# Key chunks of the memory behind the sums of the first two norms, and dense retention products set between the small S5 output products

## The reference

```python
# block 1
u = modulate(x, sh1, sc1); y = swiglu(u, ffn1_w_gate, ffn1_w_up, ffn1_w_down)
x = layer_norm(DEEPNORM_ALPHA * x + FFN_RES_WEIGHT * (1 + g1) * y, ln1_g, ln1_b)       # first norm
u = modulate(x, sh2, sc2); proj = u @ w_in     # recurrent branch, convolution branch, two gates
out = merged @ mix_w_out
x = layer_norm(DEEPNORM_ALPHA * x + (1 + g2) * out, ln2_g, ln2_b)                      # second norm
u = modulate(x, sh3, sc3); y = swiglu(u, ffn2_w_gate, ffn2_w_up, ffn2_w_down)
x = layer_norm(DEEPNORM_ALPHA * x + FFN_RES_WEIGHT * (1 + g3) * y, ln3_g, ln3_b)       # third norm
# block 2
h = rms_norm(x, norm1_g)
q, k, v, g_ret, u, g_s5 = split(h @ w_in_2)
ret = retention(rotary(q), rotary(k), v, ret_gn_g) * silu(g_ret)   # 8 heads, norm over each head
ssm = s5_branch(u, ...) * silu(g_s5)       # linear recurrence with 64 states in 64 groups, then a GLU
x = x + concatenate([ret, ssm]) @ w_out
m = rms_norm(mem, norm_mem_g)              # memory: 256 rows of 1024
ka = m @ xa_wk; va = m @ xa_wv             # keys and values: they depend on the memory alone
x = x + cross_attention(rms_norm(x, norm2_g) @ xa_wq, ka, va) @ xa_wo
return rms_norm(x, norm_f_g)
```

## Time and profile before

| | |
|---|---|
| median of 3 runs | 1992.2 us (1989.76 to 1996.63) |
| the profiled execution | 1996.91 us, of which its span is 1995.1 us |
| TensorE busy | 1895.3 us (95%) |
| VectorE, ScalarE, GpSimd busy | 1072.9, 775.2, 487.0 us |
| moved between device memory and the core | 239.43 MB, mean 120 GB/s |
| mean granted TensorE clock | 0.958 of full speed |

### The profile page before, as it was taken

One profiled execution on the slowest core, in us unless ns is written; L12 is line 12 of the kernel. 1 busy time (PEld: TensorE's weight loads), 2 busy tenths in 40 slices (PEclk: granted clock), 3 DMA queues, 4 the chain that ended last, 5 costly groups with the idle time before them and its releaser, 6 DMA issues.

```text
span 1995.1 us, 23150 instructions
## 1 busy us (share of the span) xinstructions
PE 1895.3 (95%) x8986; PEld 1537.1 (77%) x8986; DVE 1072.9 (54%) x1097; ACT 775.2 (39%) x814; POOL 487.0 (24%) x636
## 2 busy tenths in 40 slices
...
GB/s 302 137 195 173 185 169 157 155 93 85 84 126 127 74 95 148 126 85 64 105 91 98 85 108 87 146 116 192 169 54 156 96 68 46 101 173 90 152 43 43
DMA packets 202773, 239.43 MB, mean 120 GB/s; under 512 B 5611, under 2 KB 184587, under 8 KB 201547
## 3 DMA queue, kind: packets, MB, share of 16 engines
...
## 4 chain that ended last, share of the span: by engine, by line
PE 70%; POOL 9%; DVE 7%; ACT 6%; issue 5%; DMA 1%; SPq 1%; DVEq 0%; POOLq 0%; ACTq 0%
PE ps L2025 22%; PE ps L2214 16%; PE ps L2091 9%; POOL conv_out L481 8%; PE ps L2055 4%; ACT w_hi L603 3%; PE ps L2352 2%; PE ps L2393 2%; PE ps L2530 2%; DVE w_lo L1163 2%; DVE ada_acc L1263 2%; PE ps L2443 1%; PE ps L2431 1%; PE ps L2402 1%; DMA w_raw<-in_ffn_w_gate 1%
## 5 line engine op out<-in xcount | busy, mean ns | idle before, releaser
L1163 DVE TENSOR_TENSOR w_lo<-w_raw,w_hi 128x2048 fp32r<-128x2048 f32 x158 | 369.7, 2340 | 577.2 <-ACT w_hi L603 574.9
L603 ACT ACTIVATE w_hi<-w_raw 128x2048 fp32r<-128x2048 f32 x156 | 298.4, 1913 | 684.3 <-PE ps L2214 235.5
L2025 PE MATMUL ps<-u_hi,w_hi 128*128 128x512 f32 x704 | 279.8, 397 | 5.1 <-DVE w_lo L1163 5.0
L2025 PE MATMUL ps<-u_lo,w_hi 128*128 128x512 f32 x704 | 276.2, 392 | 0.0
L2025 PE MATMUL ps<-u_hi,w_lo 128*128 128x512 f32 x704 | 276.0, 392 | 0.0
L2214 PE MATMUL ps<-u_hi,w_hi 128*128 128x512 f32 x656 | 256.9, 392 | 5.0 <-DVE w_lo L1163 5.0
L2214 PE MATMUL ps<-u_lo,w_hi 128*128 128x512 f32 x656 | 255.8, 390 | 0.0
L2214 PE MATMUL ps<-u_hi,w_lo 128*128 128x512 f32 x656 | 255.8, 390 | 0.0
L481 POOL TENSOR_TENSOR conv_out<-conv_out,conv_tap 128x512 f32<-128x512 f32 x120 | 195.4, 1628 | 92.9 <-ACT conv_tap L745 75.9
L2025 PEld LDWEIGHTS ps<-u_hi,w_hi 128*128 128x128 f32 x704 | 133.7, 190 | 37.1 <-issue 7.5
L2025 PEld LDWEIGHTS ps<-u_lo,w_hi 128*128 128x128 f32 x704 | 133.7, 190 | 28.6 <-issue 1.0
...
## 6 DMA issues: line engine op xcount, KB each, us to landing
w_raw<-in_w_in SPq DMA_DIRECT2D x44, 1024.0 KB, 5.1
...
w_raw<-in_ffn_w_gate SPq DMA_DIRECT2D x22, 1024.0 KB, 5.3
w_raw<-in_ffn_w_up SPq DMA_DIRECT2D x22, 1024.0 KB, 5.3
...
ada_first<-in_ada_w SPq DMA_DIRECT2D x8, 1024.0 KB, 14.3
w_raw<-in_w_out SPq DMA_DIRECT2D x8, 1024.0 KB, 5.1
w_raw<-in_rnn_w_proj SPq DMA_DIRECT2D x4, 1024.0 KB, 5.2
```

The source lines that it names most:

```text
L603: A(WHI[:, slot], WRAW[:, slot], ACT.Copy).then_inc(s["w_hi"], 1)
L1163: V.tensor_tensor(WLO[:, slot], WRAW[:, slot], WHI[:, slot].bitcast(F32), ALU.subtract).then_inc(s["w_lo"], 1)
L2025: ins = M(PS[:, 2 * j + t, 0:n], w[:, j, at_:at_ + P], a[:, k, 0:n], start=(k == 0 and q == 0), stop=(k == KT - 1 and q == 2))
```

## The change

It has two parts.

**The memory moves forward.** Phase `wk` is cut in two: `wka` (the first two key chunks) stands after `down1`, `wkb` after `mix`. On TensorE they run behind the statistics of the first and second norm. The memory is loaded, scaled and transposed during `down1`, and split there into two new tiles (`mem_hi_made`, `mem_lo_made`). The place where the products read them, `mem_hi` and `mem_lo`, is in use by the feed-forward activations, so ScalarE stores both to device memory and loads them back at each of the three norms (`memory_reload`). In `ln_modulate_hi` and `ln_modulate_lo` the weight splits and the evacuations of the key chunks are set between the tiles. The four value chunks stay: three go in front of `norm(4)`, one behind it. The dummy activation that loads a table ahead is Ln instead of Exp.

**The S5 output is mixed with dense products.** `gate_tile` becomes `gate_part` (a range of k). The loop over heads has half a gate tile for each head; the other five halves are set between the small products of `toeplitz` and `states`, one k step (three dense products) after each quarter. In the last three of these groups stand steps of `wout_r` (`ret_part`, six dense products each). The banks of the sums of S5 change, batch 2 now also waits for a gelu. ScalarE's and VectorE's programs follow: `ret_lo` is taken out of `finish`, and `ca_batch(3)` goes behind all heads.

```diff
-PHASES = [("ffn1", 22, 11), ("down1", 16, 4), ("conf", 8, 4), ("xr", 4, 2), ("gb", 4, 2), ("ga", 4, 2), ("gr", 4, 2),
-          ("ya", 4, 2), ("yb", 4, 2), ("mix", 4, 2),
-          ("ffn2", 22, 11), ("down2", 16, 4), ("wk", 4, 2), ("wv", 4, 2), ("u", 4, 2), ("v", 4, 2), ("gs5", 4, 2),
+PHASES = [("ffn1", 22, 11), ("down1", 16, 4), ("wka", 2, 1), ("conf", 8, 4), ("xr", 4, 2), ("gb", 4, 2), ("ga", 4, 2), ("gr", 4, 2),
+          ("ya", 4, 2), ("yb", 4, 2), ("mix", 4, 2), ("wkb", 2, 1),
+          ("ffn2", 22, 11), ("down2", 16, 4), ("wv", 4, 2), ("u", 4, 2), ("v", 4, 2), ("gs5", 4, 2),
...
-        Y_BANK = (0, 4, 6, 4)
+        Y_BANK = (4, 6, 4, 6)
...
-            def ln_modulate_hi(c, at_, n_u, n_y):
-
+            def ln_modulate_hi(c, at_, n_u, n_y, ph):
+
+                hi_step(ph, 0, 2, 0)
+                kv_evac(ph, 0)
                 for f in range(KT + 1):
+                    if f == 2:
+                        kv_evac(ph, 1)
+                        half = slice(0, 4) if ph == "wka" else slice(4, 8)
+                        act.wait_ge(free[0], UB[ph] + 1)
+                        act.wait_ge(free[1], UB[ph] + 1)
+                        act.dma_start(ka_dram[:, half], KAS[:, half]).then_inc(s["kv_store"], 16)
+                        hi_step(ph, 0, 2, 1)
...
+            def down_act(ph, c, after, memory=False):
+                if memory:
                     for n in range(12):
                         hi_step(ph, n // 4, 4, n % 4)
-                        between(n)
+                        memory_act(n)
                 else:
                     split_only(ph, 4, 3)
                 hi_step(ph, 3, 4, 0)
+                if memory:
+                    act.wait_ge(s["mf_ready"], KT)
+                    A(MHM[:], MF[:], ACT.Copy).then_inc(s["mh"], 1)
                 hi_step(ph, 3, 4, 1)
                 ln_squares(c, X, 0, 4)
+                if memory:
+                    act.wait_ge(s["ml"], 1)
+                    act.wait_ge(s["mh"], 1)
+                    act.dma_start(mh_dram, MHM[:].bitcast(F32)).then_inc(s["kv_store"], 16)
+                    act.dma_start(ml_dram, MLM[:].bitcast(F32)).then_inc(s["kv_store"], 16)
                 hi_step(ph, 3, 4, 2)
-                if last:
-                    last()
+                act.wait_ge(s["mm"], CB[after] - 1)
+                if memory:
+                    act.wait_ge(s["kv_store"], 32)
+                memory_reload()
                 ln_squares(c, X, 4, 7)
-                A(EPSC[:, 4 + c:5 + c], EPSC[:, 1:2], ACT.Exp)
+                A(EPSC[:, 4 + c:5 + c], EPSC[:, 1:2], ACT.Ln)
+                hi_step(ph, 3, 4, 3)
                 ln_squares(c, X, 7, 8)
                 ln_mean_square(c)
-                if last:
-                    hi_step(ph, 3, 4, 3)
                 ln_root(c)
-                if not last:
-                    hi_step(ph, 3, 4, 3)
-            down_act("down1", 0)
-            ln_modulate_hi(0, 0, 8, 0)
+            down_act("down1", 0, "wka", True)
+            ln_modulate_hi(0, 0, 8, 0, "wka")
...
+            act.wait_ge(s["mm"], CB["mix"])
+            memory_reload()
...
+            gate_silu(0)
+            gate_silu(1)
+            hi_step("gret", 0, 2, 0)
+            head(0)
+            head(1)
+            gate_silu(2)
+            head(2)
+            head(3)
+            gate_silu(3)
+            hi_step("gret", 0, 2, 1)
+            head(4)
+            head(5)
+            gate_silu(4)
+            head(6)
+            head(7)
+            gate_silu(5)
...
+            y_evac(0)
+            hi_step("gret", 1, 2, 0)
+            gate_silu(6)
             toeplitz(2)
-            y_evac(0)
-            ret_hi(0)
-            ret_hi(1)
+            y_evac(1)
+            gate_silu(7)
+            for h in range(4):
+                ret_hi(h)
             toeplitz(3)
-            y_evac(1)
-            ret_hi(2)
-            ret_hi(3)
-            y_evac(2)
+            hi_step("gret", 1, 2, 1)
             ret_hi(4)
             ret_hi(5)
-            y_evac(3)
+            y_evac(2)
             ret_hi(6)
             ret_hi(7)
+            hi_step("wout_r", 0, 2, 0)
+            y_evac(3)
...
+            def memory_lo():
+                dve.wait_ge(s["mh"], 1)
+                V.tensor_tensor(MLM[:], MF[:], MHM[:].bitcast(F32), ALU.subtract).then_inc(s["ml"], 1)
...
             ca_batch(0)
+            ca_batch(1)
             dve.wait_ge(s["rroot"], 1)
             V.reciprocal(RSTDH[:], RSTDH[:]).then_inc(s["rn"], 1)
-            ca_batch(1)
             finish(0)
             finish(1)
-            ca_batch(2)
+            lo_step("gret", 1, 2, 0)
             finish(2)
             finish(3)
+            ca_batch(2)
+            for h in range(4):
+                ret_lo(h)
+            for h in (4, 6):
+                finish(h)
+                finish(h + 1)
+                ret_lo(h)
+                ret_lo(h + 1)
+            lo_step("gret", 1, 2, 1)
...
+            def key_chunk(ph, j, loaded):
+                pe.wait_ge(s["mem_load"], loaded)
+                gemm_chunk(ph, 0, j, MH, ML, MEM)
+
+            gemm_down("down1", 0, 0, True, memory_t)
             ln_stats(0, X, 7, True)
+            key_chunk("wka", 0, 48)
+            key_chunk("wka", 1, 48)
...
+            key_chunk("wkb", 0, 80)
+            key_chunk("wkb", 1, 80)
...
-            for n in range(4):
-                key_chunk(n)
+            for n in range(3):
+                value_chunk(n)
             norm(4)
-            value_chunk(0)
             pe.wait_ge(s["s5_expand"], 4)
             T(PS[:, 5, 0:96], SROW[0:96], IDENT[0:96, 0:96]).then_inc(s["s5_t"], 1)
-            for n in range(1, 4):
-                value_chunk(n)
+            value_chunk(3)
...
+            def gate_part(f, first, last):
                 n, j, t = f // 2, f // 2 % 2, f % 2
-                pe.wait_ge(s["w_lo"], CB["gret"] + n + 1)
-                pe.wait_ge(free[t if f >= 2 else 0], UB["gret"] + f // 2)
-                q = 0
-                for k in range(KT):
-                    for w, a in ((WHI, UH), (WHI, UL), (WLO, UH)):
+                if first == 0:
+                    pe.wait_ge(s["w_lo"], CB["gret"] + n + 1)
+                    pe.wait_ge(free[t if f >= 2 else 0], UB["gret"] + f // 2)
+                for k in range(first, last):
+                    for q, (w, a) in enumerate(((WHI, UH), (WHI, UL), (WLO, UH))):
                         at_ = 256 * k + P * t
-                        ins = M(PS[:, t], w[:, j, at_:at_ + P], a[:, k], start=(q == 0), stop=(q == 3 * KT - 1))
-                        q += 1
-                ins.then_inc(s["mm"] if t else s["gate_mm"], 1)
+                        ins = M(PS[:, t], w[:, j, at_:at_ + P], a[:, k], start=(k == 0 and q == 0), stop=(k == KT - 1 and q == 2))
+                if last == KT:
+                    ins.then_inc(s["mm"] if t else s["gate_mm"], 1)
...
             for h in range(1, HEADS):
+                gate_part(2 + (h - 1) // 2, (4, 0)[h % 2], (8, 4)[h % 2])
                 if h + 1 < HEADS:
-                    gate_tile(h + 1)
                     scores(h + 1)
                 head_output(h)
                 variance(h - 1)
...
+                    if r == 7:
+                        ins.then_inc(s["mb_used"], 1)
+                    if r % 2:
+                        dense(r // 2)
...
+            def ret_part(j, k):
+
+                if k == 0:
+                    pe.wait_ge(s["w_lo"], CB["wout_r"] + j + 1)
+                    pe.wait_ge(free[0], UB["wout_r"])
+                    pe.wait_ge(free[1], UB["wout_r"])
+                pe.wait_ge(s["rl"], HEADS if j else k + 1)
+                for t in range(2):
+                    for q, (w, a) in enumerate(((WHI, UH), (WHI, UL), (WLO, UH))):
+                        at_ = 256 * k + P * t
+                        ins = M(PS[:, 2 * j + t], w[:, j, at_:at_ + P], a[:, k],
+                                start=(k == 0 and q == 0), stop=(k == KT - 1 and q == 2))
+                if k == KT - 1:
+                    ins.then_inc(s["mm"], 1)
...
+            toeplitz(0, lambda k: gate_part(5, 4 + k, 5 + k))
             variance(HEADS - 1)
-            toeplitz(1)
-            states(0)
+            states(0, lambda k: gate_part(6, k, k + 1))
+            toeplitz(1, lambda k: gate_part(6, 4 + k, 5 + k))
             spread(0)
             spread(1)
-            pe.wait_ge(s["o_ready"], HEADS)
-            toeplitz(2)
-            states(1)
+            states(1, lambda k: gate_part(7, k, k + 1))
             spread(2)
             spread(3)
-            states(2)
+            pe.wait_ge(s["o_ready"], HEADS)
+            toeplitz(2, lambda k: gate_part(7, 4 + k, 5 + k))
             spread(4)
             spread(5)
-            toeplitz(3)
-            states(3)
+            states(2, lambda k: ret_part(0, k))
             spread(6)
             spread(7)
-            pe.wait_ge(s["y_gelu"], 1)
```

(7 more changed lines are left out.)

226 lines of the change are left out of this document (112 added, 114 removed).

## The result

The changed kernel takes 2000.4 us (median of 20 runs) where the kernel before takes 1989.8 (20 runs on the same chip). The ratio is 1.005, 95% interval 1.0032 to 1.0068: slower by half a per cent, where 1963 was forecast. The others scatter from 1986 to 2015.

The account below looks back on a forecast made before the run. TensorE, busy for 95% of the span, was taken as the bound through its idle time, slow clock and work. The terms -9 - 3.5 + 22.5 + 19 = 29 took 1992.2 to 1963 us, with an 8-in-10 range of 1947 to 1984.

Parts of the forecast that it names:

- First norm, -9: Norm after the first feed-forward block: squares 4 to 6 wait for the memory's stores and reload, losing 9 us.
- Second norm, -3.5: Norm after the mix: reload hidden by mix products, key chunks fill the gap, the pair ends later, losing 3.5 us.
- Third norm to `u`, +22.5: Third norm to S5 input product: shorter ScalarE and VectorE chain starts the third `u` chunk 22.5 us earlier; bounds 16, 27.
- S5 output, +19: S5 output stage: shorter loop over heads and dense products between small ones at full clock start `glu` earlier, gaining 19 us.
- the last small product is at T + 72: S5 output: at full clock, small products end 72 us after T, the start of the first Toeplitz product.
- Hidden, with 3 us of cover: S5 output: GpSimd's recurrence ends before the first state products need it, with 3 us to spare.
- Dense products between them are meant to hold it: S5 output: dense products set between the small ones keep TensorE's clock at full, 1.00 instead of 0.50.
- Rival (b): S5 output: clock stays at half through the mixed stage, y comes 51 us later than forecast, 2014 us; chance 10%.

Follow-up runs that it names:

- e2: Kernel before with only the mixed S5 output, the memory left as before: 2001.3 us, ratio 1.0037 to the kernel before.
- e3: Changed kernel with the second Toeplitz product and half a gate set ahead of the first state product: 1992.4 us, ratio 0.9997 to the kernel before.
- e14: Kernel before plus the memory's move, first key chunks reading the memory where it was split, spreads over 128 rows (120 zero): 1960.6 us, ratio 0.9835.
- e11: e3 with spreads over 128 rows (120 zero), y stored in two parts and first key chunks reading the split memory in place: 1967.7 us, ratio 0.9869.
- e12: Changed kernel in its own order, only the spreads over 128 rows (120 zero) instead of 8: 1990.1 us, ratio 0.9977 to the kernel before.
- e1: Kernel before with only the memory's move, the S5 output unmixed: 1984.4 us, ratio 0.996 to the kernel before.
- e13: Kernel before with only the spreads over 128 rows (120 zero) instead of 8: 1976.1 us, ratio 0.9916.

## Why the prediction was wrong

- **First norm, -9: right, measured -9.8.** The pair ends at 485.7 against 475.9, and squares 4 to 6 stand behind a DMA. The statistics end at 447.0, not 444; the key chunks took 11.9 us at nearly full clock instead of 13.5, which made up for a part.
- **Second norm, -3.5: right in kind, measured about -5** (14.0 late at 945.5, of which 8.6 came in with the statistics). The pair took 28.9 us, where 26.8 was forecast: the waits for tiles stayed. During `ffn2` and `down2` 2.5 us came back; the memory's transposes that had stood there are the likely reason.
- **Third norm to `u`, +22.5: right in kind, measured 27.3,** just above the upper bound of 27. The third chunk of `u` starts 15.8 earlier although `down2` ended 11.5 later. Of this 2.6 went to the low clock behind the 4.80 us wait. At T the gain is 13.1 besides the 13.6 moved; 10 was forecast.
- **S5 output, +19: the step that failed.** I had `glu` at T + 113.3, measured T + 143.5. Two terms of that sum held: from the issue of the y stores to the use of their reload 30.8 us passed (30.7 forecast), and from there to `glu` 7.5 (7.6). What failed is "the last small product is at T + 72": it ends at T + 103.8. Of these 32 us, waits make up 3 (5.0 for the recurrence and 2.0 for C A, 4 forecast), the clock 26.8, and 2 stay unexplained.
- **"Hidden, with 3 us of cover".** I took the recurrence's end from the trace of before, and did not ask what VectorE would do beside it once T came earlier. C A now ran beside the last two steps; they took 10 us more. In e2, where the recurrence was 1 us ahead of C A, there was no wait.
- **"Dense products between them are meant to hold it".** Between Toeplitz and state quarters they do (e2, e3). They don't hold it behind the spreads, and I never asked which of the stage's products mattered. e14 shows that with the spreads on 128 rows the mix gains nothing: from T to `glu` e14 takes 95.1 us, and e11 117.8, or 104.2 without the moved 13.6.
- **The base was misread.** The row at 1773.83 is VectorE's addition; the first product of `glu` stands at 1769.4 in the trace of before. So 4.4 of the 19 never existed.
- **Rival (b), 10%, had the mechanism:** the clock at half, a loss of 51 us in the stage. The clock cost about half of that, 26.8. The range (1947 to 1984) left it out. The rule cited from the Trainium skill, "TensorE: Matmul & The Clock Gate", section "HAM oscillation — how this bites in real kernels", that idle gaps of TensorE throttle it, has its part (the gap ahead of states 0, the first stretch of e12), but not the whole: in e3 the clock fell with TensorE busy for 13.00 of 13.00 us on both sides.

Account at `glu`, in the traces: +26.7 at T, less 29.6 in the stage, is 2.9 later, and 0.7 comes behind it; the spans differ by 3.6. Against the 29 forecast that is a miss of 32.6: 30.2 in the stage, 4.4 for the misread base, 0.7 behind `glu`, less the 3.1 that T came earlier than forecast; the rest is rounding. The miss of the medians is 37.4, and the further 5 us are differences between executions.

What stays open: why 8 rows. The runs show that spreads over 128 rows instead of 8 decide, with the same count of products and columns and the same duration (1.98 us for two spreads of 8 rows, 1.99 of 128). They don't show what the chip looks at, nor what 120 moving rows of zeros would do. Also open is what makes one low stretch end after 20 us and another after 60, and what makes the first fall in the unmixed stage (before, e1, e14). It stands 2.4 us behind the end of the one wait of 1.10 us, which follows the last variance, a product with 8 columns of weights (`head_columns`). No run of the unmixed stage changed either, and e13 has both without a fall there.
